# A decoder step with a 32-expert MoE: gathering the routed tokens in slot order, and copying out the windows of experts 0 and 1 in between

## The chip, the core and the metric

The kernel runs on one core of one Trainium2 chip. The metric is the device time of one execution in microseconds. Before the change three runs took 748.0, 749.03 and 749.11 us, with a median of 749.03 us. All of the kernel works on float32 data. Where it wants matmul precision it splits a value into a rounded high part (type fp32r) and the low remainder, and adds three products (high by high, low by high, high by low).

## The reference, cut to what matters

304 tokens (16 meta tokens and 256 prompt tokens, 8 times 4 sample tokens) of 1024 channels pass a mixer, and then a mixture of 32 experts in 4 groups. Only the mixture matters here:

```python
def _hier_moe(xn, ...):
    gidx = top_k(gl, 1)                      # one group of 4 for each token
    ev, eidx = lax.top_k(el_sel, 2)          # two experts of the 8 in the group
    combine = one_hot(flat_idx) * weights    # two weights for each token
    for e in range(N_EXPERTS):               # 32
        he = silu(xf @ w_exp_gate[e]) * (xf @ w_exp_up[e])   # 1024 -> 256, twice
        y = y + combine[:, e:e + 1] * (he @ w_exp_down[e])   # 256 -> 1024
```

## The kernel before, in words

**Stages.** The mixer takes the first 358 us of the span. Then come the router (logits, ranks, positions), the selection, the 32 experts, and a tail that picks each token's two result rows from memory, adds them and normalises.

**Slots.** Each token goes to two experts, so there are SLOTS = 608 pairs. The pairs are laid out by expert: expert 0's tokens first, then expert 1's. An expert has at most C = 96 slots in one pass. `off_i` holds the slot at which each expert's tokens begin.

**Selection** (PE: function `gathers`, line 1460). A 0/1 matrix `sel` (304 tokens in 3 row tiles by 608 slots, made by VectorE at lines 1167 and 1168) is multiplied with the normalised tokens, so that slot columns come out as `xs`, 8 channel chunks by 608 slots. A chunk of 304 columns, half of the slots, fits one PSUM bank, so there are 16 steps q: 8 channel chunks by 2 halves. Each step takes 6 matmuls (3 token tiles, high and low part). The steps use banks 0 to 3 in turn. The first four steps run tile by tile as `sel` arrives; step q from 4 on waits (`gat_done`, line 1480) until ScalarE has copied step q - 4 out. ScalarE's copy (line 803) multiplies by the norm's gain and writes `xs`. Before the change, q // 2 is the channel chunk and q % 2 the half, so an expert's columns are complete only after the last step.

**Windows.** An expert's 96 columns, all 8 chunks, are then copied from `xs` at the slot read from `off_i` (a register load, line 785) as `xe_hi` on ScalarE (`window`, line 788), and VectorE subtracts to get `xe_lo` (line 1203, helper line 1189). There are two buffers of each, by e % 2. Before the change, `sel` lies in the same memory as the two `xe_hi` buffers, so these can't be written while a gather still reads `sel`.

**Weights.** For each expert SyncE loads gate, up and down, 1 MB each, into a ring of 4 slots. ScalarE rounds gate and up into `hi_gu[e % 2]` (`split_gate_up`, line 777, two halves), VectorE subtracts into `lo_gu` (line 1189). The same is done to one half of down (`split_down`).

**Order around the change.** Each engine has a list written out by hand, and waits in order:

- ScalarE: `split_gate_up(0)`, `split_down(0)`, `split_gate_up(1)`, the 16 copies, two register loads, `window(0)`, `window(1)`, then the loop over experts, where each turn starts with Silu of the gate (line 814).
- VectorE: a wait for `sel`, `split_gate_up(0)`, `split_down(0)`, `split_gate_up(1)`, `window(0)`, `window(1)`, then the loop, where each turn starts with the product of Silu and up (`hid`, line 1215).
- PE: the gathers, then `gate_up(0)` (line 1498, 24 matmuls of 512 columns), `turn(0)` (two transposes of `hid`, line 1510), `gate_up(1)`, `down(0)` (line 1523), `turn(1)`, `gate_up(2)`, and so on. `gate_up(0)` and `gate_up(1)` wait for all 16 copies (`gat_done`, line 1492), for the expert's `xe_lo` (line 1493) and for its `lo_gu` (line 1496).
- SyncE: expert 3's weights once the last gather is done (line 382), and expert e + 4's gate and up once `gate_up(e)` is done (line 387).

Of the kernel before, what the change touches and what calls it, by code (L numbers as in the profile page):

```python
# [9 lines left out]
ACT = mybir.ActivationFunctionType  # L10
# [8 lines left out]
KT = D // P  # L19
# [4 lines left out]
T = TP + NS * TS  # L24
ROWS = (P, P, T - 2 * P)
NT = len(ROWS)
# [12 lines left out]
SLOTS = 2 * T  # L39
# [12 lines left out]
LRU_C = 8.0  # L52
WORK = 19616
MAX_PASSES = -(-T // C)
PLACE_STEPS = 17
ST_DMAS = 6 + NS
WO_BANKS = (0, 1, 2, 3, 6, 7)
# [4 lines left out]
GU_WORDS = KT * 2 * F  # L62
# [20 lines left out]
def trunk(nc, a, o):  # L83
    with ExitStack() as ctx:
# [9 lines left out]
        def rounded(name, buf, at, n):  # L94

            return nc.alloc_sbuf_tensor_at(name, [P, n], F32R, offset=start[buf] + 4 * at)[:, :]
# [4 lines left out]
        bank = [ctx.enter_context(nc.psum_tensor(f"bank{i}", [P, 512], F32))[:, :] for i in range(8)]  # L101
# [4 lines left out]
        work = sb("work", WORK)  # L106
# [38 lines left out]
        xs, xT2 = chan(xs_f), chan(xs_f[:, 0:KT * T])  # L145
        at_hi = KT * XS
# [4 lines left out]
        junk = work[:, at_hi + D:at_hi + 2 * D]  # L151
        at_xe = at_hi + 2 * GU_WORDS + 2 * D
        xe_hi = [rounded(f"xe_hi{b}", "work", at_xe + b * KT * C, KT * C).rearrange("p (k n) -> p k n", k=KT) for b in range(2)]
        sel = rounded("sel", "work", at_xe, NT * SLOTS).rearrange("p (t n) -> p t n", t=NT)
        cut(NT * SLOTS)
        logit = cut((NG + NE) * NT).rearrange("p (t e) -> p t e", t=NT)
        el, oh1, oh2, rank, inw, rtmp = (cut(NE * NT).rearrange("p (t e) -> p t e", t=NT) for _ in range(6))
# [55 lines left out]
        g2_row = par[:, KT * (NG + NE):KT * (NG + NE) + KT]  # L213
# [332 lines left out]
        def _(act):  # L546
# [197 lines left out]
            for t in range(NT + 1):  # L744
# [6 lines left out]
                j = 2 * t + 1  # L751
# [18 lines left out]
            def experts(r):  # L770

                def split_gate_up(e):
                    s = e % EXP_SLOTS
                    act.wait_ge(gu_in[s], r * (32 * NE // EXP_SLOTS) + 32 * (e // EXP_SLOTS) + 32)
                    for q in range(2):
                        k = slice(q * HK, q * HK + HK)
                        nc.scalar.activation(hi_gu[e % 2][:, k], w_gu[s][:, k], ACT.Copy).then_inc(ehi_gu, 1)  # L777

                def split_down(e):
                    s = e % EXP_SLOTS  # L780
                    act.wait_ge(dn_in[s], r * (16 * NE // EXP_SLOTS) + 16 * (e // EXP_SLOTS) + 16)
                    nc.scalar.activation(hi_dn[e % 2], w_dn[s][:, 0], ACT.Copy).then_inc(ehi_dn, 1)

                def first_token(e):
                    return act.value_load(off_i[0:1, e:e + 1], min_val=0, max_val=SLOTS)

                def window(e, at):
                    nc.scalar.activation(xe_hi[e % 2], xs[:, :, bass.ds(at, C)], ACT.Copy).then_inc(xe_act, 1)  # L788

                def results(e):  # L790
                    act.wait_ge(dn_mm, r * NE + (e + 1))
                    if e:
                        act.wait_ge(row_out, r * (16 * NE) + 16 * e)
                    for n in range(2):
                        ins = nc.scalar.activation(row_st[:, n * 512:(n + 1) * 512], bank[4 + n][0:C], ACT.Copy)  # L795
                    ins.then_inc(row_done, 1)

                split_gate_up(0)
                split_down(0)
                split_gate_up(1)  # L800
                for q in range(2 * KT):
                    act.wait_ge(gat_mm, r * (2 * KT) + (q + 1))
                    nc.scalar.activation(xs[:, q // 2, (q % 2) * T:(q % 2 + 1) * T], bank[q % 4][:, 0:T],
                                         ACT.Copy, scale=g2_row[:, q // 2:q // 2 + 1]).then_inc(gat_done, 1)
                at = [first_token(e) for e in range(2)]
                act.wait_ge(gat_done, r * (2 * KT) + 2 * KT)
                act.wait_ge(tail_done, 1)
                for e in range(2):
                    window(e, at[e])
                for e in range(NE):  # L810
                    act.wait_ge(gu_mm, r * NE + (e + 1))
                    if e:
                        act.wait_ge(hid_done, r * NE + e)
                    nc.scalar.activation(sg2, bank[e % 2][0:C, 0:F], ACT.Silu).then_inc(silu2, 1)
                    if e + 2 < NE:
                        split_gate_up(e + 2)
                    act.wait_ge(th_mm, r * NE + (e + 1))
                    nc.scalar.activation(hT_hi, bank[2][:, 0:C], ACT.Copy)
                    nc.scalar.activation(hT_f, bank[2][:, C:2 * C], ACT.Copy).then_inc(hT_act, 1)
                    if e:  # L820
                        results(e - 1)
                    if e + 2 < NE:
                        window(e + 2, first_token(e + 2))
                    if e + 1 < NE:
                        split_down(e + 1)
                results(NE - 1)
# [24 lines left out]
        def _(dve):  # L851
# [43 lines left out]
            e, z, z2, q = lam[:, 0], lam[:, 3], lam[:, 4], lam[:, 1]  # L895
# [14 lines left out]
            for s in range(NS):  # L910
                dve.wait_ge(cst_T, s // 2 + 1)
                at = GLP + s * GLS
# [205 lines left out]
            for t in range(NT):  # L1118
                ins = vec.scalar_tensor_tensor(logit[0:ROWS[t], t], bank[(5, 6, 7)[t]][0:ROWS[t], 0:NG + NE],
                                               stat[0:ROWS[t], 9 + t:10 + t], rbias[0:ROWS[t]], ALU.mult, ALU.add)  # L1120
# [64 lines left out]
            def experts(r):  # L1185

                def split(part, whole, high, done, n, out_done):
                    dve.wait_ge(done, n)
                    vec.tensor_tensor(part, whole, as_f32(high), ALU.subtract).then_inc(out_done, 1)  # L1189

                def split_gate_up(e):
                    s = e % EXP_SLOTS
                    for q in range(2):
                        k = slice(q * HK, q * HK + HK)
                        split(lo_gu[s][:, k], w_gu[s][:, k], hi_gu[e % 2][:, k], ehi_gu, r * (2 * NE) + (2 * e + q + 1), elo_gu)

                def split_down(e):
                    s = e % EXP_SLOTS
                    split(lo_dn[s], w_dn[s][:, 0], hi_dn[e % 2], ehi_dn, r * NE + (e + 1), elo_dn)

                def window(e):
                    at = dve.value_load(off_i[0:1, e:e + 1], min_val=0, max_val=SLOTS)
                    split(xe_lo[e % 2], xs[:, :, bass.ds(at, C)], xe_hi[e % 2], xe_act, r * NE + (e + 1), xe_dve)

                dve.wait_ge(sel_done, r * NT + NT)
                split_gate_up(0)
                split_down(0)
                split_gate_up(1)
                window(0)
                window(1)  # L1210
                for e in range(NE):
                    dve.wait_ge(silu2, r * NE + (e + 1))
                    if e:
                        dve.wait_ge(th_mm, r * NE + e)
                    vec.tensor_tensor(hid, bank[e % 2][0:C, F:2 * F], sg2, ALU.mult).then_inc(hid_done, 1)
                    if e + 2 < NE:
                        split_gate_up(e + 2)
                    dve.wait_ge(hT_act, r * NE + (e + 1))
                    vec.tensor_tensor(hT_lo, bank[2][:, 0:C], as_f32(hT_hi), ALU.subtract).then_inc(hT_dve, 1)
                    if e + 2 < NE:  # L1220
                        window(e + 2)
                    if e + 1 < NE:
                        split_down(e + 1)
# [56 lines left out]
        def _(pe):  # L1280
# [179 lines left out]
            def gathers(r):  # L1460

                def gather(q, t):

                    n = ROWS[t]
                    for part in (xn2_hi, xn2_lo):
                        ins = mm(bank[q % 4][:, 0:T], part[t][0:n].rearrange("p (m j) -> p j m", j=KT)[:, q // 2],  # L1466
                                 sel[0:n, t, (q % 2) * T:(q % 2 + 1) * T],
                                 start=(t == 0 and part is xn2_hi), stop=(t == NT - 1 and part is xn2_lo))
                    return ins

                pe.wait_ge(hi_done, r * NT + NT)
                pe.wait_ge(lo_done, r * NT + NT)
                for t in range(NT):
                    pe.wait_ge(sel_done, r * NT + (t + 1))
                    for q in range(4):
                        ins = gather(q, t)
                        if t == NT - 1:
                            ins.then_inc(gat_mm, 1)
                for q in range(4, 2 * KT):
                    pe.wait_ge(gat_done, r * (2 * KT) + (q - 3))  # L1480
                    for t in range(NT):
                        ins = gather(q, t)
                    ins.then_inc(gat_mm, 1)
# [79 lines left out]
```

## Time and profile before

| what | value |
|---|---|
| median of 3 runs | 749.03 us (748.0 to 749.11) |
| the profiled execution | 748.74 us |
| its span in the trace | 747.0 us, so 1.74 us lie around the span |
| mean granted clock of PE | 0.911 of full speed |
| PE busy | 665.1 us, 89% of the span |
| VectorE busy | 539.4 us, 72% |
| ScalarE busy | 368.1 us, 49% |
| DMA | 160.29 MB, 215 GB/s over the span |

Starts are counted in us from the span's start. A wait stands in square brackets behind the instruction that waited, with the time and what ended it. PEld is the weight load in front of a matmul. The granted clock is 1.00 at 2.4 GHz and 0.50 at 1.2 GHz. Ends of matmuls are modelled, so the distance between the starts of two of them is the safer reading.

### The profile page before, as it was taken

To read this page: it belongs to the slowest core of one execution; us is meant where nothing else is said; L and a number is where in the kernel's file an instruction comes from. 1 tells how busy PE (TensorE), PEld (TensorE's weight loads), DVE (VectorE), ACT (ScalarE), POOL (GpSimd) and SP (SyncE) were. 2 spreads that over 40 slices of the span, in tenths; PEclk is the share of its full clock that TensorE was granted. 3 is DMA by queue.
4 is the path that set the end of the run, shared out by engine and by line. 5 is a ranking of instruction groups with operands and counts; after the bars stand their busy time and mean duration, and the time that the engine had idled before them with its cause. 6 is when DMAs were issued, how large, how long until landed. Compare 5 with 4: busy or idle time off the path is not lost.

```text
span 747.0 us, 8243 instructions
## 1 busy us (share of the span) xinstructions
PE 665.1 (89%) x3004; PEld 497.6 (67%) x3004; DVE 539.4 (72%) x739; ACT 368.1 (49%) x515; POOL 134.8 (18%) x102
## 2 busy tenths in 40 slices
PE   5999998992976979999999899999999999999920
PEld 5677776771966879987697566666666666666610
DVE  2079987898999999752287067877788888887406
ACT  2120115443721516540263267778777778778421
POOL 1019852062674500210000000000000000000030
PEclk8699999996897989999686599999999999999975
DMA  9756053333041323440700379999999999998143
GB/s 269 212 179 225 7 219 113 112 113 113 23 149 55 117 109 124 134 169 0 309 29 0 120 291 365 397 399 396 398 403 409 396 395 406 402 395 314 43 148 123
DMA packets 46054, 160.29 MB, mean 215 GB/s; under 512 B 7566, under 2 KB 10870, under 8 KB 33702
## 3 DMA queue, kind: packets, MB, share of 16 engines
q1 hardware_dynamic: 37152, 153.99, 54.5%
q10 hardware_dynamic: 8150, 3.21, 2.1%
q0 software_dynamic: 704, 2.49, 1.0%
q8 instruction: 26, 0.43, 0.2%
q14 instruction: 22, 0.18, 0.1%
HBM read 145.51 MB, written 15.02 MB: 215 GB/s over the span
## 4 chain that ended last, share of the span: by engine, by line
PE 55%; DVE 5%; issue 2%; DMA 1%; ACT 1%; POOL 0%; POOLq 0%; DVEq 0%; ACTq 0%
PE bank L1498 24%; PE bank L1523 13%; PE bank L1414 4%; PE bank L1466 4%; PE bank L1344 4%; PE bank L1286 2%; PE bank L1429 1%; DVE w_lo L995 1%; DMA ring<-expert_rows,row_i 1%; PE bank L1510 1%; PE bank L1441 1%; DVE x L1261 1%; DVE conv L1037 1%; DVE gel_lo L995 0%; DVE work L990 0%
## 5 line engine op out<-in xcount | busy, mean ns | idle before, releaser
L1189 DVE TENSOR_TENSOR lo_gu<-ring,hi_gu 128x2048 fp32r<-128x2048 f32 x64 | 143.8, 2288 | 39.9 <-ACT hi_gu L777 39.9
L1349 PE MATMUL bank<-work,ring 128*128 128x304 f32 x512 | 135.5, 426 | 1.0 <-ACT work L576 1.0
L927 DVE SCALAR_TENSOR_TENSOR work<-work,par 128x272 f32<-128x272 f32 x240 | 131.7, 620 | 0.0
L1349 PEld LDWEIGHTS bank<-work,ring 128*128 128x128 f32 x512 | 98.8, 193 | 35.8 <-issue 3.0
L777 ACT ACTIVATE hi_gu<-ring 128x2048 fp32r<-128x2048 f32 x64 | 118.5, 1901 | 0.0
L1498 PE MATMUL bank<-hi_gu,xe_hi 128*96 128x512 f32 x256 | 103.9, 406 | 3.6 <-issue 3.6
L1498 PE MATMUL bank<-lo_gu,xe_hi 128*96 128x512 f32 x256 | 101.6, 397 | 0.0
L1498 PE MATMUL bank<-hi_gu,xe_lo 128*96 128x512 f32 x256 | 101.2, 395 | 0.0
L530 POOL DMA_INDIRECT ring<-expert_rows,row_i x6 | 5.7, 953 | 346.7 <-DMA expert_rows<-outst 345.2
L1344 PE MATMUL bank<-xn_hi,w_hi 128*128 128x304 f32 x128 | 41.7, 326 | 26.6 <-DVE xn_lo L995 15.1
L1523 PE MATMUL bank<-ring,windows 128*96 128x512 f32 x128 | 65.3, 591 | 0.0
L1498 PEld LDWEIGHTS bank<-hi_gu,xe_hi 128*96 128x96 f32 x256 | 42.7, 167 | 19.8 <-issue 3.9
L453 POOL TENSOR_TENSOR work<-ring 128x272 f32<-128x272 f32 x8 | 45.8, 5722 | 52.4 <-ACT ring L602 52.4
L1498 PEld LDWEIGHTS bank<-lo_gu,xe_hi 128*96 128x96 f32 x256 | 41.5, 162 | 18.7
L1498 PEld LDWEIGHTS bank<-hi_gu,xe_lo 128*96 128x96 f32 x256 | 41.9, 164 | 16.1
L995 DVE TENSOR_TENSOR w_lo<-ring,w_hi 128x2048 fp32r<-128x2048 f32 x17 | 40.2, 2370 | 14.7 <-ACT w_hi L657 14.7
L657 ACT ACTIVATE w_hi<-ring 128x2048 fp32r<-128x2048 f32 x20 | 38.1, 1909 | 20.8 <-PE bank L1344 9.7
L1189 DVE TENSOR_TENSOR xe_lo<-work,xe_hi 128x768 fp32r<-128x768 f32 x32 | 30.4, 952 | 20.4 <-ACT xe_hi L788 20.2
L1344 PEld LDWEIGHTS bank<-xn_hi,w_hi 128*128 128x128 f32 x128 | 26.7, 208 | 27.5 <-issue 27.5
L795 ACT ACTIVATE outst<-bank 96x512 f32<-96x512 f32 x64 | 34.6, 592 | 17.6 <-DMA expert_rows<-outst 13.9
L1344 PE MATMUL bank<-xn_lo,w_hi 128*128 128x304 f32 x128 | 41.4, 323 | 0.0
L1344 PE MATMUL bank<-xn_hi,w_lo 128*128 128x304 f32 x128 | 41.1, 321 | 0.0
(271 smaller groups left out, 1167.7 us busy)
## 6 DMA issues: line engine op xcount, KB each, us to landing
ring<-w_exp_gate SPq DMA_DIRECT2D x32, 1024.0 KB, 7.1
ring<-w_exp_up SPq DMA_DIRECT2D x32, 1024.0 KB, 9.4
ring<-w_exp_down SPq DMA_DIRECT2D x32, 1024.0 KB, 9.5
ring<-w_in SPq DMA_DIRECT2D x11, 2048.0 KB, 8.3
expert_rows<-outst SPq DMA_DIRECT2D x32, 384.0 KB, 7.6
ring<-w_rnn_proj SPq DMA_DIRECT2D x2, 2048.0 KB, 7.7
ring<-w_conv_proj SPq DMA_DIRECT2D x2, 2048.0 KB, 8.3
ring<-w_out SPq DMA_DIRECT2D x2, 2048.0 KB, 7.6
```

The source lines that it names most:

```text
L453: nc.gpsimd.tensor_tensor(glu[:, c, CW - 1:GLP], cv_sb[:, c % 2, 0:TP], sg_sb[:, c % 2, 0:TP], ALU.mult)
L657: nc.scalar.activation(hi, w, ACT.Copy).then_inc(whi_done, 1)
L777: nc.scalar.activation(hi_gu[e % 2][:, k], w_gu[s][:, k], ACT.Copy).then_inc(ehi_gu, 1)
L795: ins = nc.scalar.activation(row_st[:, n * 512:(n + 1) * 512], bank[4 + n][0:C], ACT.Copy)
L927: ins = vec.scalar_tensor_tensor(y, glu[:, ch, w:w + TP], pcw[:, w, ch:ch + 1], y, ALU.mult, ALU.add)
L995: vec.tensor_tensor(part, value, as_f32(high), ALU.subtract).then_inc(lo_sem, 1)
L1189: vec.tensor_tensor(part, whole, as_f32(high), ALU.subtract).then_inc(out_done, 1)
L1344: ins = mm(bank[m % 4][:, 0:T], w[:, i, cols], xp[i], start=(i == 0 and j == 0), stop=(i == KT - 1 and j == 2))
L1349: ins = mm(bank[m % 4][:, 0:T], mix_w[b % MIX_SLOTS][:, i, (c % MB) * P:(c % MB + 1) * P], xnT[:, i], start=(i == 0), stop=(i == KT - 1))
L1414: ins = mm(bank[q][0:ROWS[t]], xp[:, c, tok], w[:, i], start=(c == 0 and j == 0), stop=(c == KT - 1 and j == 2))
L1498: ins = mm(bank[b][0:C], xp[b][:, k], w[:, k], start=(k == 0 and j == 0), stop=(k == KT - 1 and j == 2))
L1523: ins = mm(bank[4 + n][0:C], hp, w[:, at], start=(j == 0), stop=(j == 3))
```

## The change

The gathers take all 8 channel chunks of the first half of the slots in steps 0 to 7, and those of the second half in steps 8 to 15. `sel` moves from the memory of the `xe_hi` buffers to that of `hi_gu[1]`. ScalarE copies out the windows of experts 0 and 1 behind its copies 9 and 12, each after a wait for the first 8 copies. ScalarE's `split_gate_up(1)` moves behind all 16 copies, since `hi_gu[1]` holds `sel` until then, and the wait for `tail_done` (the zeroed end of `xs`) moves behind that. VectorE's `window(0)` moves ahead of its `split_gate_up(1)`.

```diff
+FIRST_WINDOWS = (9, 12)
...
-        sel = rounded("sel", "work", at_xe, NT * SLOTS).rearrange("p (t n) -> p t n", t=NT)
+        sel = rounded("sel", "work", at_hi + GU_WORDS, NT * SLOTS).rearrange("p (t n) -> p t n", t=NT)
...
                 split_gate_up(0)
                 split_down(0)
-                split_gate_up(1)
                 for q in range(2 * KT):
                     act.wait_ge(gat_mm, r * (2 * KT) + (q + 1))
-                    nc.scalar.activation(xs[:, q // 2, (q % 2) * T:(q % 2 + 1) * T], bank[q % 4][:, 0:T],
-                                         ACT.Copy, scale=g2_row[:, q // 2:q // 2 + 1]).then_inc(gat_done, 1)
-                at = [first_token(e) for e in range(2)]
-                act.wait_ge(gat_done, r * (2 * KT) + 2 * KT)
+                    nc.scalar.activation(xs[:, q % KT, (q // KT) * T:(q // KT + 1) * T], bank[q % 4][:, 0:T],
+                                         ACT.Copy, scale=g2_row[:, q % KT:q % KT + 1]).then_inc(gat_done, 1)
+                    if q in FIRST_WINDOWS:
+                        e = FIRST_WINDOWS.index(q)
+                        at = first_token(e)
+                        act.wait_ge(gat_done, r * (2 * KT) + KT)
+                        window(e, at)
+                split_gate_up(1)
                 act.wait_ge(tail_done, 1)
-                for e in range(2):
-                    window(e, at[e])
...
                 split_down(0)
+                window(0)
                 split_gate_up(1)
-                window(0)
                 window(1)
...
-                        ins = mm(bank[q % 4][:, 0:T], part[t][0:n].rearrange("p (m j) -> p j m", j=KT)[:, q // 2],
-                                 sel[0:n, t, (q % 2) * T:(q % 2 + 1) * T],
+                        ins = mm(bank[q % 4][:, 0:T], part[t][0:n].rearrange("p (m j) -> p j m", j=KT)[:, q % KT],
+                                 sel[0:n, t, (q // KT) * T:(q // KT + 1) * T],
```

## Rows read from the trace of the kernel before

**Rows 1.** The page: PE's busy line, and its granted clock in 40 slices

```profile
PE 665.1 (89%) x3004; PEld 497.6 (67%) x3004; DVE 539.4 (72%) x739; ACT 368.1 (49%) x515; POOL 134.8 (18%) x102
...
PEclk8699999996897989999686599999999999999975
```

**Rows 2.** Chain that ended last, 380 to 460 us: start, length, engine, line

```profile
390.49 32.26 PE bank L1466 x96
...
422.77 0.52 ACT work L803
423.29 3.02 issue
426.32 7.63 PE bank L1498 x24
...
433.97 0.39 ACT gate_weights L814
...
434.38 0.43 DVE gate_weights L1215
...
435.34 5.56 PE bank L1498 x24
```

**Rows 3.** Timeline of ScalarE: start, length, line, operation, count, wait before it

```profile
389.63 3.70 ACT L777 ACTIVATE hi_gu<-ring 128x2048 fp32r<-128x2048 f32 x2
...
409.80 0.51 ACT L803 ACTIVATE work<-bank,par 128x304 f32<-128x304 f32 x1 [1.65 <-PE bank L1466]
411.96 0.51 ACT L803 ACTIVATE work<-bank,par 128x304 f32<-128x304 f32 x1 [1.65 <-PE bank L1466]
414.12 0.51 ACT L803 ACTIVATE work<-bank,par 128x304 f32<-128x304 f32 x1 [1.65 <-PE bank L1466]
...
424.28 1.58 ACT L788 ACTIVATE xe_hi<-work 128x768 fp32r x2 [0.99 <-ACT work L803]
```

**Rows 4.** Timeline of VectorE

```profile
401.88 4.48 DVE L1189 TENSOR_TENSOR lo_gu<-ring,hi_gu 128x2048 fp32r<-128x2048 f32 x2
...
425.26 1.83 DVE L1189 TENSOR_TENSOR xe_lo<-work,xe_hi 128x768 fp32r<-128x768 f32 x2 [18.90 <-ACT xe_hi L788]
...
436.18 4.49 DVE L1189 TENSOR_TENSOR lo_gu<-ring,hi_gu 128x2048 fp32r<-128x2048 f32 x2 [1.38 <-ACT hi_gu L777]
```

**Rows 5.** Timeline of PE's weight loads in one gather step

```profile
407.53 1.03 PEld L1466 LDWEIGHTS bank<-sel,half 128*128 128x128 f32 x4 [0.27 <-issue]
```

**Rows 6.** Timeline of PE in the first gate_up: matmuls 2 and 10

```profile
426.83 0.63 PE L1498 MATMUL bank<-hi_gu,xe_lo 128*96 128x512 f32 x1
...
430.24 0.45 PE L1498 MATMUL bank<-hi_gu,xe_hi 128*96 128x512 f32 x1
```

**Rows 7.** Stretches of PE alone: us, busy (count), granted clock, DMA share, GB/s

```profile
230.27:235.40 5.13, 5.13 (x20) 0.50 0.01 3
235.40:235.90 0.50, 0.50 (x5) 0.62 0.00 0
263.88:269.50 5.62, 5.62 (x22) 0.50 0.55 210
269.50:270.00 0.50, 0.50 (x4) 0.58 0.00 0
...
426.32:430.00 3.68, 3.68 (x9) 0.50 1.02 427
430.00:430.40 0.40, 0.40 (x3) 0.57 0.92 389
```

**Rows 8.** One stretch, all engines: PE, PEld, DVE, ACT, POOL, clock, DMA, GB/s

```profile
462.25:702.15 239.90, 239.90 (x973) 154.53 (x972) 190.85 (x162) 186.54 (x242) 0.00 (x0) 1.00 0.96 377
```

**Rows 9.** Waits of SyncE's DMA queue, 420 to 711 us

```profile
SPq L358 <- PE bank L1498: 86.2, 28, 9.9
```

**Rows 10.** DMA issues, 480 to 560 us and 640 to 690 us: median us to landing

```profile
ring<-w_exp_up SPq DMA_DIRECT2D x9, 1024.0 KB, 9.5
...
ring<-w_exp_up SPq DMA_DIRECT2D x4, 1024.0 KB, 9.2
```

## The prediction

> **What bounds the kernel now.** I read the page first: PE is busy 89% of the span, and its granted clock dips several times, the last of them before the tail at the router and the gathers [rows 1]. Then the chain that ended last, around the selection. From 390.49 us it runs over PE alone: 96 gather matmuls for 32.26 us, then ScalarE's last copy of 0.52 us, then 3.02 us in which the chain names nothing ("issue"), then the first gate_up at 426.32 us [rows 2]. What stands in the 3.02 us is seen in the timelines: ScalarE sits 0.99 us between its last copy and the windows (register loads and a semaphore), makes the two windows from 424.28 us in 1.58 us, and VectorE's `xe_lo` of expert 0 begins at 425.26 us, a pair of them taking 1.83 us [rows 3, 4]. So the windows stand between the gathers and the experts while PE does nothing. After that PE works without a pause: 239.90 us busy of 239.90 us between 462.25 and 702.15 us [rows 8]. Whatever is taken from PE's path ahead of that stretch comes off the end, if nothing gives it back.
>
> **The change, part by part.** The sum is made for the profiled execution, 748.74 us (747.0 us of span and 1.74 us around it); the median of the runs is 0.29 us above it.
>
> *Windows taken off the path.* Expert 0 has at most 96 slots and begins at 0; expert 1 begins by 96, so both windows end by column 192, inside the first half of 304. They are complete after copy 7. `gate_up(0)` then waits only for the last copy, which ends at 423.29 us [rows 2]. How long PE takes from there is a handoff. The trace gives one from ScalarE to VectorE of 0.02 us (433.97 plus 0.39 to 434.38), and the pause of PE's weight loads at a gather step, where the awaited copy was done long before, of 0.27 us [rows 2, 5]. PE has three waits, all but the first met by then. I take 0.10 us, nearer to the first since the gathers' pause comes with a pile of weight loads; the ends are 0.02 and 0.30. PE starts at 423.39 instead of 426.32 us: **-2.9 us** (-3.0 to -2.7).
>
> *The windows' new place.* In the gathers a step takes 2.16 us (0.51 of copy and 1.65 of waiting on ScalarE [rows 3]). Step 9's copy starts at 409.80 us. Behind it come a register load and a window: at most 0.99 us (which held two loads before) and about 0.85 us, since two windows took 1.58. ScalarE is back by 412.2 us, where the next copy was due at 409.80 + 2.16 = 411.96 us: 0.2 us late. PE needs that bank only four steps after it was filled, so three steps cover it, over 6 us. The copy of step 12 starts three steps later, and by the last copy ScalarE is on time: 0. Without this cover the two would cost 2 times 0.2 us. VectorE's `window(0)` falls into its 18.90 us of waiting [rows 4]: 0.
>
> *`split_gate_up(1)` behind the gathers.* On ScalarE it leaves 389.63 us, where it delayed nothing (the first copies wait for PE), and begins at 423.29 us. Two halves take 3.70 us, to 427.0; VectorE follows after the first, 1.9 us later (3.70 over 2), at 425.2 us, takes 4.49 us, to 429.7, and `window(1)` adds 0.95 us (half of 1.83, rounded up), to 430.6 [rows 3, 4]. What hides it is `gate_up(0)`, 7.63 us. From 423.39 it ends at 431.0; Silu and `hid` follow as before, with VectorE wanted for `hid` 0.43 us after that (426.32 + 7.63 to 434.38 [rows 2]), at 431.5. VectorE is free 0.9 us earlier. Behind the moved work on ScalarE stands Silu, which can't begin before 431.0 either, 4 us after ScalarE is done; behind it on VectorE stands only `hid`. `gate_up(1)` starts 1.4 us after the end of `gate_up(0)`, 1.8 us after `window(1)` is done. Cost 0; if the cover were gone (ScalarE's 3.70, VectorE's last half of 2.25 and 0.95 in the open after `gate_up(0)`) it would be 6.9 less 1.4 us.
>
> *The order of the gathers, and `sel`'s place.* The same 96 matmuls, shapes and banks, only other chunks of the same tiles. In the old order every second step repeats the chunk of the step before; step 10 brings a new one and step 11 repeats it, and both copies come 2.16 us after the one before (409.80, 411.96, 414.12 [rows 3]). So a new chunk in every step costs nothing and gains nothing: 0. No row shows `sel` at another address; with the same reads of it, 0 as well.
>
> *SyncE.* Expert 3's weights still leave after the last gather; loads 4 and later follow `gate_up` and shift with it. Nothing is passed on a queue.
>
> *The clock.* PE runs at 0.50 through the gathers and into `gate_up(0)`. In the stretch from 430.00 to 430.40 us the mean is 0.57, so the rise came 0.06 us before its end, at 430.34 (0.07 of the 0.50 between the levels, times 0.40 us), 4.02 us after the first matmul [rows 7]. At the low level a matmul takes (430.24 - 426.83) / 8 = 0.426 us, at the high one 5.56 / 24 = 0.232 us [rows 6, 2], so each us of low clock costs 1 - 0.232/0.426 = 0.46 us. I take the same 4.02 us after the new start. Two other starts after idle time rose later: 235.78 less 230.27 is 5.51 us, 269.92 less 263.88 is 6.04 us [rows 7]. At 6.04 us, 2.02 later, it would cost 0.9 us. An earlier rise can gain at most 0.9 us too, since then `hid` waits for VectorE, which is free at 430.6 only.
>
> Sum: 748.74 - 2.9 = 745.8 us for the profiled execution, **746.1 us** against the median.
>
> **The rule weighed against it.** The forecast ties the rise to the start of the dense work; the rows show a rise 4.02, 5.51 and 6.04 us after three such starts, so it is not one fixed delay [rows 7]. The Trainium skill (TensorE: Matmul & The Clock Gate, section "Part 1: The HAM clock gate", "What's actually happening") says that the watch on PE's activity runs freely and does not start anew with a kernel, so that the point of the rise varies. By that rule the three unequal delays are what one would see, and an earlier start need not bring an earlier rise.
>
> **Rivals.**
>
> 1. *The rise stays where it was, at 430.34 us.* Then `gate_up(0)` runs 430.34 - 423.39 = 6.95 us low instead of 4.02: 2.93 times 0.46 = 1.35 us given back, a gain of 1.6, **747.5 us**. For it: the unequal delays. Against: 6.95 us is longer than each of the three delays seen. The Trainium skill (TensorE: Matmul & The Clock Gate, the section named above) would allow it.
>
> 2. *VectorE becomes the bound.* If its chain runs 1.8 us later than worked out (it would start after both of ScalarE's halves, at 427.0), it ends at 432.4 and `hid` begins 0.9 us late: **747.0 us**. Against: VectorE's pair follows ScalarE's first half after 1.38 us of waiting in the expert loop, half by half [rows 4].
>
> 3. *DMA sets the pace of the experts, and gives the gain back:* **749.0 us**, no change. For it: the DMA share is 0.96 at 377 GB/s over the expert stretch [rows 8]. Against: SyncE waits 86.2 us for PE over 28 loads, so PE's progress releases them, and the time to landing does not grow along the stage, 9.5 then 9.2 us [rows 9, 10]; PE has no idle time there [rows 8].
>
> 4. *Slower: the clock does not rise in `gate_up(0)` at all.* All 24 matmuls at 0.426 take 10.2 us, 2.6 more than 7.63; after the 1.4 us pause `gate_up(1)` starts low as well, and 4.02 us at 0.46 costs 1.8 more. With the gain of 2.9 that is +1.5 us, **750.6 us**. It decides from a rise later than 4.02 + 2.9/0.46 = 10.3 us after the start, about when `gate_up(0)` would end. For it: the gathers leave the clock low, and they now run up to 0.6 us before the dense work. Against: the rise came in 4 to 6 us each time.
>
> That the change doesn't do what it says is ruled out by the columns: both windows lie in the first half.
>
> **How the numbers follow.** Chances: the forecast, with the rise 3 to 6 us after the start, 0.74; rival 1 0.10; rival 2 0.07; rival 3 0.06; rival 4 0.03. The forecast's own ends: 746.1 less 0.9 (early rise) and 0.1 (handoff) is 745.1; plus 0.9 (late rise) and 0.2 (handoff) is 747.2. Rival 1's 747.5 is taken in, so the range is 745.1 to 747.5; half of rival 1, rivals 3 and 4 and some scatter (the runs of before lie within 1.1 us) stay outside. A measurement of this kernel tells about 0.2%, 1.5 us, from no change, so the border is 747.5: the forecast, rival 2 and half of rival 1 lie under it, 0.86, of which 0.01 goes off for scatter: 0.85 for faster; rival 3, the other half and the scatter are the same, 0.12; rival 4 is slower, 0.03.
>
> **What would show it.** In the changed trace: the copies of steps 9 and 12 followed by one window each, the next copy late by some 0.2 us and no wait of PE for it; between the last copy and the first line-1498 matmul 0.1 us instead of 3.02; `lo_gu` of expert 1 and its `xe_lo` done on VectorE before `hid`; the rise of the clock some 4 us behind the new start; PE without idle time in the experts, and the tail as long as before. It would be wrong if the gathers took longer than 32.3 us, if idle time showed ahead of the first Silu, `hid` or `gate_up(1)`, or if waits on expert loads appeared.

## The result, and the profile after

The first comparison gave a median of 743.42 us over 6 runs (742.28 to 745.31) against 748.05 us for the kernel before (6 runs, 747.17 to 749.11), a ratio of 0.994 with a 95% interval of 0.9921 to 0.9958. The change is faster, as forecast, but the time lies below the range of 745.1 to 747.5 us. The profiled execution took 742.31 us, with a span of 740.6 us.

The chain of waits of the changed kernel from the gathers to the second expert (start, length, engine, line), the answer to [rows 2]. Lines 1466, 1498, 814 and 1215 of the kernel before are 1468, 1500, 816 and 1217 here:

```profile
388.49 31.89 PE bank L1468 x96
...
420.40 0.52 ACT work L803
420.92 0.04 issue
420.97 7.45 PE bank L1500 x24
...
428.50 0.39 ACT gate_weights L816
...
428.91 0.43 DVE gate_weights L1217
...
429.87 5.56 PE bank L1500 x24
```

The 3.02 us of "issue" have become 0.04. That is the whole of what the change sets out to do, and it is done. But the first gather starts at 388.49 us and not at 390.49, after code that the change does not touch. The difference of the two spans, 6.4 us, splits like this: 2.0 ahead of the first gather, 0.4 in the gathers, 3.0 in the pause, 0.2 in the first gate_up, and 0.9 behind the start of the second one (747.0 - 435.34 = 311.7 before, 740.6 - 429.87 = 310.7 after). Only the third of these was forecast. Each is the difference of one profile and another; further profiles of both kernels follow below.

ScalarE's timeline in the changed kernel, the answer to [rows 3] (step 9, its window, steps 10 to 12, the second window, steps 13 to 15, and `split_gate_up(1)`):

```profile
407.42 0.51 ACT L803 ACTIVATE work<-bank,par 128x304 f32<-128x304 f32 x1 [1.65 <-PE bank L1468]
408.32 0.84 ACT L789 ACTIVATE xe_hi<-work 128x768 fp32r x1 [0.39 <-ACT work L803]
409.59 0.52 ACT L803 ACTIVATE work<-bank,par 128x304 f32<-128x304 f32 x1 [0.42 <-PE bank L1468]
...
414.56 0.84 ACT L789 ACTIVATE xe_hi<-work 128x768 fp32r x1
416.07 0.51 ACT L803 ACTIVATE work<-bank,par 128x304 f32<-128x304 f32 x1 [0.67 <-PE bank L1468]
...
420.40 0.51 ACT L803 ACTIVATE work<-bank,par 128x304 f32<-128x304 f32 x1 [1.65 <-PE bank L1468]
420.81 3.70 ACT L778 ACTIVATE hi_gu<-ring 128x2048 fp32r<-128x2048 f32 x2
```

Behind the first window ScalarE still waits 0.42 us for PE: the next copy is on time, since one register load leaves 0.39 us of idle time and not 0.99. VectorE's answer to [rows 4]:

```profile
422.75 4.49 DVE L1191 TENSOR_TENSOR lo_gu<-ring,hi_gu 128x2048 fp32r<-128x2048 f32 x2 [12.48 <-ACT hi_gu L778]
427.16 0.95 DVE L1191 TENSOR_TENSOR xe_lo<-work,xe_hi 128x768 fp32r<-128x768 f32 x1
428.91 0.42 DVE L1217 TENSOR_TENSOR gate_weights<-bank,gate_weights 96x256 f32<-96x256 f32 x1 [0.80 <-ACT gate_weights L816]
```

VectorE waits 0.80 us for Silu ahead of `hid`: the moved split is hidden, where 0.9 us of room had been worked out. The expert stage is as before (240.00 us busy of 240.00 us on PE), the answer to [rows 8]:

```profile
424.00:424.80 0.80, 0.80 (x4) 0.51 (x3) 0.80 (x1) 0.52 (x1) 0.00 (x0) 0.65 1.04 430
...
456.77:696.77 240.00, 240.00 (x974) 154.57 (x974) 190.97 (x162) 186.68 (x243) 0.00 (x0) 1.00 0.95 376
```

The first row of that fence answers to [rows 7]: a mean clock of 0.65 over 0.80 us puts the rise at 424.80 less 0.24, 424.56 us, 3.59 us after the first matmul of gate_up, where 4.02 was taken.

So the question of the study is the 1.7 us between the 2.9 forecast and the 4.6 measured. Two theories stood against each other. **Scatter**: the change is worth its pause, and the rest is where the clock happens to rise and fall in stretches that it does not touch. **Local**: the change itself gains 4 to 5 us.

### The profile page after: what moved, and what is told of

It reads as the page before. It is cut to its first block, busy times and chain, and to the rows that moved or that the text cites. A ratio compares the mean times of both kernels' runs of the same rounds, so it can differ in the third digit from the quotient of the medians.

```text
span 740.6 us, 8243 instructions
## 1 busy us (share of the span) xinstructions
PE 659.3 (89%) x3004; PEld 492.8 (67%) x3004; DVE 539.8 (73%) x739; ACT 368.2 (50%) x515; POOL 135.8 (18%) x102
## 4 chain that ended last, share of the span: by engine, by line
PE 59%; DVE 3%; DMA 1%; issue 1%; ACT 0%; POOL 0%; POOLq 0%; DVEq 0%; ACTq 0%
PE bank L1500 24%; PE bank L1525 14%; PE bank L1346 7%; PE bank L1416 5%; PE bank L1468 4%; PE bank L1288 2%; PE bank L1431 1%; DMA ring<-expert_rows,row_i 1%; PE bank L1512 1%; PE bank L1443 1%; DVE x L1263 1%; DVE conv L1039 1%; DVE gel_lo L997 0%; DVE x L1277 0%; POOL ring L531 0%
## 5 line engine op out<-in xcount | busy, mean ns | idle before, releaser
L1191 DVE TENSOR_TENSOR lo_dn<-ring,hi_dn 128x1024 fp32r<-128x1024 f32 x32 | 39.0, 1218 | 1.7 <-ACT hi_dn L783 1.7
L1346 PE MATMUL bank<-xn_hi,w_lo 128*128 128x304 f32 x128 | 39.9, 312 | 0.0
```

What stands on the lines that cost most here:

```text
L1346: ins = mm(bank[m % 4][:, 0:T], w[:, i, cols], xp[i], start=(i == 0 and j == 0), stop=(i == KT - 1 and j == 2))
```

## Experiments

### The two kernels again

The kernel before, run again as if it were a change:

> The kernel before, unchanged, with a profile of its own. Scatter theory (the change is worth 2.9 us at the handoff, the rest of the 4.6 us measured is where the granted clock happens to rise and fall in stretches the change does not touch): ratio 1.000, single times scattered over 1 to 3 us as in the runs before; the first gather starts at another time than 390.49 us, by up to 2 us, and the stretch from the first gather to the end of the first gate_up is 43.5 us within 1. Local theory (the change itself is worth 4 to 5 us, between the first gather and the end of the first gate_up): the first gather starts within 0.3 us of 390.49 and the stretch is 43.5 us within 0.3.

Measured: 748.36 us (745.65 to 750.12, 12 runs), ratio 1.0009 (0.9994 to 1.0023). Its first gather starts at 389.59 us, 0.9 us ahead of the same code in the profile before, and 43.4 us pass from there to the end of the first gate_up.

> The changed kernel, unchanged, with a profile of its own. Scatter theory: ratio 0.9955 to 0.9965 (2.6 to 3.4 us); the pause between the last copy and the first gate_up 0.05 us; the stretch from the first gather to the end of the first gate_up 40.5 us within 1; the start of the first gather not tied to 388.5 us. Local theory: ratio 0.993 to 0.995 (4 to 5 us), the stretch below 39.5 us, and the first gather as in the kernel before.

Measured: 745.34 us (742.16 to 748.13, 10 runs), ratio 0.9957 (0.9941 to 0.9974), which is 3.2 us. The chain of its profile:

```profile
390.33 32.28 PE bank L1468 x96
...
422.63 0.52 ACT work L803
423.15 0.04 issue
423.20 7.42 PE bank L1500 x24
```

The pause is 0.04 us here too, but the first gather starts at 390.33 us: the 2 us ahead of the gathers did not come from the change. A third comparison of both:

> The changed kernel a third time. Scatter theory: ratio 0.9945 to 0.9965, so that over all its runs it stays at 3.0 to 3.6 us; the profile has a pause of 0.05 us ahead of the first gate_up, and single times spread over 3 us or more. Local theory: ratio 0.9925 to 0.9945, as the 4.6 us of the first comparison.

Measured: 745.45 us (743.78 to 747.74, 12 runs), ratio 0.9972 (0.9957 to 0.9987): less than expected, on the other side of the forecast from the first comparison. Its pause is 0.04 us again, its first gather at 390.57 us.

> The kernel before a third time, as a measure of the scatter. Scatter theory: ratio 1.000 within 0.0015, single times over 3 us or more; its first gather starts between 388 and 391 us, and a span is short where that start is early. Local theory: the first gather at 390.5 within 0.3.

Measured: 747.31 us (745.37 to 749.19), ratio 0.9995 (0.998 to 1.001), first gather at 390.18 us. Its pause and the gate_up behind it:

```profile
422.45 0.52 ACT work L803
422.97 3.02 issue
425.99 7.66 PE bank L1498 x24
```

All runs of the two kernels in this study (119 of the kernel before, those beside the experiments below among them, and 28 of the changed one) have means of 747.90 and 745.03 us: **2.9 us**. Standard deviations of single runs are 1.4 and 1.5 us, so that difference is uncertain by some 0.6 us (twice the root of 1.4 squared over 119 plus 1.5 squared over 28). By the means of each comparison for itself it is 4.5, 2.8 and 2.0 us; the two repeats together, without the first that they were to check, give 2.4. The intervals of the first and the third comparison barely touch, so one comparison is somewhat less certain than its own interval says.

The traces measure the change with less of that scatter. From the first gather to the end of the first gate_up it takes 43.5, 43.4 and 43.5 us in the three profiles of the kernel before, and 39.9, 40.3 and 40.4 in those of the changed one: 3.2 us less, within what the scatter theory said (40.5 within 1) and above the 39.5 that the local theory allowed. The local theory falls by this.

### The parts of the change, one at a time

The order of gathers and copies alone, on the kernel before:

```diff
-  xs[:, q // 2, (q % 2) * T:...]   and   j=KT)[:, q // 2], sel[0:n, t, (q % 2) * T:...]
+  xs[:, q % KT, (q // KT) * T:...] and   j=KT)[:, q % KT], sel[0:n, t, (q // KT) * T:...]
```

> The order of the gathers and of their copies alone; sel, the windows and the splits stay where they were. Scatter theory: ratio 1.000 within 0.002, gather stretch 32.3 us within 0.9, pause ahead of the first gate_up 3.0 us. A rival, that the new order itself makes the gathers cheaper (a fresh chunk at each step): ratio 0.998 or less, and the gathers under 31.4 us.

Measured: ratio 0.9992 (0.9976 to 1.0008), gathers 32.14 us, pause 3.02 us. The order alone is worth nothing that can be told.

The changed kernel with the windows behind the copies again:

```diff
-                    if q in FIRST_WINDOWS:
...
-                        window(e, at)
-                split_gate_up(1)
-                act.wait_ge(tail_done, 1)
+                at = [first_token(e) for e in range(2)]
+                act.wait_ge(gat_done, r * (2 * KT) + 2 * KT)
+                act.wait_ge(tail_done, 1)
+                for e in range(2):
+                    window(e, at[e])
+                split_gate_up(1)
```

> The changed kernel, with the two windows put back behind the 16 copies, and split_gate_up(1) behind them. Scatter theory: the 3.0 us pause is back, split_gate_up(1) stays hidden under the first gate_up; ratio to the kernel before 1.000 within 0.002. Rival, that moving sel and split_gate_up(1) is itself worth something: ratio 0.998 or less; rival, that the moved split costs: ratio above 1.002 with VectorE late for hid.

Measured: ratio 0.9998 (0.9982 to 1.0014). Its chain:

```profile
388.57 31.86 PE bank L1467 x96
...
420.97 3.02 issue
423.99 7.63 PE bank L1499 x24
```

The pause is back and the gain is gone, though this profiled execution is a short one (745.58 us) with an early first gather, at 388.57 us. So an early start of the gathers happens without the change's windows as well. The windows' place is the part that counts; order and memory only allow it.

The windows five and three steps later:

```diff
-FIRST_WINDOWS = (9, 12)
+FIRST_WINDOWS = (14, 15)
```

> The changed kernel with the two windows behind copies 14 and 15 instead of 9 and 12. Cover theory (a window costs nothing as long as it ends ahead of the next copy's due time): the window of expert 0 fits between copies 14 and 15, that of expert 1 stands behind the last copy and pushes split_gate_up(1) back by 1.2 us, so that VectorE is 0.3 us late for hid: ratio to the kernel before 0.9955 to 0.997, as the changed kernel within its scatter. Rival, that a window between the copies holds up the gathers: the last gather 0.5 us or more later than in the changed kernel, counted from the first.

Measured: ratio 0.9953 (0.9935 to 0.997), as the changed kernel; from the first gather to the start of the last copy it takes 32.3 us (422.63 - 390.33), as in the repeats of the changed kernel, so a window between the copies holds up nothing in the gathers. But expert 0's `xe_lo` now ends at 423.31 us (422.35 and 0.96), 0.17 behind the last copy, and the first gate_up starts at 423.41 us, 0.27 behind it instead of 0.04. The cover of the split is used up, as its chain shows:

```profile
428.47 1.90 issue
430.37 0.95 DVE xe_lo L1191
431.32 0.34 DVE gate_weights L1217
```

VectorE's `window(1)` now stands in the chain directly ahead of `hid`; with Silu over at 431.20 us (430.82 and 0.38) it is late by about 0.1 us, less than the 0.3 expected.

### The pause itself

Four copies of no use ahead of the windows of the kernel before:

```diff
+                for i in range(4 if isinstance(r, int) else 0):
+                    nc.scalar.activation(xe_hi[i % 2], xs[:, :, 0:C], ACT.Copy).then_inc(extra, 1)
+                    act.wait_ge(extra, i + 1)
                 for e in range(2):
                     window(e, at[e])
```

> The kernel before with four useless copies of windows, one after the other, ahead of the two that count, so that the pause behind the gathers is about 4 us longer (0.85 us and a semaphore each). Theory that PE's pause costs its own length and no more: ratio 1.0045 to 1.006, first gate_up 7.4 to 8.5 us as before. Rival, that a longer pause also makes the clock rise later: ratio above 1.006 and a first gate_up over 8.5 us. Rival, that a pause is given back in the expert stage: ratio below 1.003.

Measured: 752.19 us, ratio 1.0057 (1.004 to 1.0074), 3.0 to 5.5 us slower. The pause grew from 3.02 to 6.54 us, that is by 3.52:

```profile
424.06 6.54 issue
430.60 8.12 PE bank L1502 x24
```

The interval holds the 3.5 us, and the first gate_up of 8.12 us is what the order-only kernel had too (426.40 to 434.52 us) behind a pause of 3.02. So a longer pause costs its length; that it costs some tenths more by a later rise of the clock is not excluded by that interval.

The other way round, PE kept at work in the pause of the kernel before:

```diff
                     ins.then_inc(gat_mm, 1)
+                keep_clock(7, 12)
```

> The kernel before, with 12 small matmuls of no use behind the last gather, so that PE works through most of the 3.0 us pause. Theory that the pause costs its own length only: the first gate_up starts at the same distance from the last gather, and the ratio is 1.000 to 0.997, the latter where the clock rises within the filled pause and the first gate_up takes 5.6 us instead of 7.6. Rival, that an idle pause in itself holds the clock down longer: the first gate_up at 5.6 to 6.2 us every time and ratio 0.997 or less, which would be 1.4 to 2 us that the change gains beside the pause.

Measured: ratio 0.9993 (0.9976 to 1.001). Its chain, and PE's clock in the filled stretch:

```profile
388.65 31.84 PE bank L1466 x96
420.49 4.81 PE bank L1286 x24
425.30 5.57 PE bank L1499 x24
```

```profile
420.42:424.00 3.58, 3.58 (x18) 0.50 0.66 227
424.00:425.06 1.06, 1.06 (x10) 0.76 0.98 410
```

The small matmuls (24 on PE, two for each of the 12) took 4.81 us, 1.3 longer than the pause and the copy together (3.54), and gate_up took 2.1 us less. The clock rose at about 424.5 us, some 4.1 us after the filling began, as late as it does behind the start of a gate_up. So the rise came some 4 us behind the start of this work, ahead of gate_up. What this leaves, 0.8 us, is within the interval; the experiment does not settle whether the idle time adds a few tenths to the delay.

### Where single runs differ

Useless matmuls at the start of the changed kernel, 40 instead of 24, so that the clock might stay up until the first tiles:

```diff
-            keep_clock(2, 24)
+            keep_clock(2, 40)
```

> The changed kernel with 40 instead of 24 small matmuls of no use at the very start, which fill PE's 6 us of waiting ahead of the first transposes. Scatter theory (single times differ because the clock rises sooner or later at several starts, of which the one at 25 us is the first): if the clock stays at 1.00 up to 25 us, the first tiles run at the high level from their start, the first gather comes 1.5 to 2.4 us earlier and the ratio to the kernel before is 0.992 to 0.995. Rival: the transposes and waits between 16 and 25 us let the clock fall all the same, and the ratio is that of the changed kernel, 0.9955 to 0.997.

Measured: ratio 0.9954 (0.9936 to 0.9971), as the changed kernel. The clock was at 0.50 from 16 us on all the same, under the transposes: the rival holds, and this run says nothing for or against the scatter theory.

What does show a source of the scatter is the router stage of three profiles, all with the same instructions there. Its transposes in the changed kernel, in the same kernel again, and in the order-only kernel (shortest, median and longest in ns, then the first and the last start):

```profile
L1443 PE MATMUL bank<-ident,x x24: 274/339/477, 358.2 to 369.3; 128*128 128x128 f32 x16, 48*128 48x48 f32 x8
```

```profile
L1443 PE MATMUL bank<-ident,x x24: 274/357/477, 358.8 to 370.8; 128*128 128x128 f32 x16, 48*128 48x48 f32 x8
```

```profile
L1441 PE MATMUL bank<-ident,x x24: 274/375/477, 357.7 to 370.3; 128*128 128x128 f32 x16, 48*128 48x48 f32 x8
```

The stage takes 30.3, 31.5 and 33.0 us up to the first gather (388.49, 390.33 and 390.70). PE's clock in it, in the same order (from 360 to 365 and from 375 to 380 us; the fourth number):

```profile
360.00:365.00 5.00, 5.00 (x29) 0.81 1.02 428
...
375.00:380.00 5.00, 5.00 (x39) 0.82 0.01 3
```

```profile
360.00:365.00 5.00, 5.00 (x25) 0.69 1.00 421
...
375.00:380.00 5.00, 5.00 (x29) 0.60 0.01 5
```

```profile
360.00:365.00 5.00, 5.00 (x22) 0.50 1.01 424
...
375.00:380.00 5.00, 5.00 (x26) 0.50 0.00 0
```

The later the clock falls and the earlier it rises, the shorter the stage, by up to 2.7 us, about the whole spread between the profiles. The other profiles of kernels with this stage agree, twelve in all: where the clock's mean from 375 to 380 us is 0.82 or 0.83, the first gather starts at 388.49 to 388.65 us (three: the changed kernel's first, and the kernels with the late windows and with the filled pause, which have the windows behind the gathers); at 0.56 to 0.69 it starts at 389.59 to 390.57 (six), and at 0.50 at 390.70 to 391.40 (three). The gathers follow too: 31.84 to 31.89 us in the first three, 32.12 to 32.31 in the others. So the 2.0 and the 0.4 us of the first pair of profiles come without the change as well. Other sources of the scatter, some 1.5 us ahead of 190 us and about 1 us behind the second gate_up (2 us more in the filled kernel's profile, where the tail's fetch of result rows and the wait ahead of it were longer), were not followed up.

### A version that beats both

The gathers' weight loads read every eighth value of a token. Writing the normalised tokens chunk by chunk makes them neighbours:

```diff
-  nc.scalar.activation(xn2_hi[t][0:n], x[0:n, t], ACT.Copy, ...
+  nc.scalar.activation(xn2_hi[t][0:n].rearrange("p (j m) -> p m j", j=KT),
+                       x[0:n, t].rearrange("p (m j) -> p m j", j=KT), ACT.Copy, ...
...
-  part[t][0:n].rearrange("p (m j) -> p j m", j=KT)[:, ...]
+  part[t][0:n].rearrange("p (j m) -> p j m", j=KT)[:, ...]
```

(`xn2_lo` likewise.) First on the kernel before:

> The kernel before, with the normalised tokens written chunk by chunk, so that a gather's weight load reads 128 neighbouring values instead of every eighth. Theory that the strided weight load paces the gathers (0.337 us of load for each of 96) and that its gaps are what let the clock fall: load 0.20 us, clock stays at 1.00, gathers 14 to 16 us instead of 32.3, first gate_up 5.6 us, ratio 0.973 to 0.980. Rival, that the load's length is set by something else than its stride: gathers 32 us, ratio 1.000.

Measured: 738.23 us, ratio 0.9861 (0.9834 to 0.9887). Then on the changed one:

> The changed kernel with the same chunk-by-chunk tokens. If the pause and the weight load are separate costs: ratio to the kernel before 0.969 to 0.976. With gathers of 15 us and a first gate_up of 5.6 us the cover of split_gate_up(1) is gone: VectorE should end window(1) about 1.3 us after hid wants it, so the gain over the dense kernel before is 1 to 2 us instead of 3. Rival: the split stays hidden and the gain over it is 3 us or more.

Measured: 736.28 us (732.44 to 737.38), ratio **0.9834** (0.9803 to 0.9864), 2.0 us by the medians below the dense kernel before (3.1 by the means, uncertain by some 2 us, so that six runs each do not tell the expected 1 to 2 us from 3). Its profile is that of its fastest run, 732.44 us. Weight loads of the gathers in this kernel, and the chain:

```profile
L1470 PEld LDWEIGHTS bank<-sel,half x96: 182/187/192, 391.4 to 409.6; 128*128 128x128 f32 x64, 48*128 48x128 f32 x32
```

```profile
391.49 18.59 PE bank L1470 x96
410.11 0.53 ACT work L804
410.68 7.37 PE bank L1502 x24
```

A load takes 0.187 us where it took 0.337, the gathers 18.6 us where they took 32.3, and the clock stays at 1.00 from 395 to 410 us, where it was 0.50 from 400 on. The clock is not what made the strided load long: in the kernel before it took 0.337 us on average from 388 to 396 us, at 1.00, and 0.332 from 400 to 420, at 0.50. Both gains were expected larger. The loads still fill the steps (1.12 us for six in a step of 1.16), and the scattered writing costs 2.03 us instead of 1.13 for each of ScalarE's three high parts and 2.00 instead of 1.28 for each of VectorE's low parts, which also read the high part at that step, on the way to the gathers. That the split's cover would be gone did not come about: the clock fell once more behind the gathers, gate_up took 7.37 us, and VectorE had 0.72 us left.

## Why the prediction was right in its mechanism and wrong in its time

**Windows off the path: right.** 2.9 us was forecast for the pause; it fell from 3.02 to 0.04 us in three profiles of three, so 2.98. The handoff taken at 0.10 us was 0.04. With the windows put back the gain is gone. That the gain of all runs, 2.9 us, agrees with the forecast to the tenth is luck: it is uncertain by 0.6, the repeats alone give 2.4, and the traces 3.2.

**The windows' new place: right.** The 0.2 us of delay came from counting two register loads; one copy later ScalarE was waiting for PE.

**The split's cover: right**, 0.80 us against 0.9, and used up where the split starts 1.2 us later.

**The clock in the first gate_up: right within its bounds.** The rise came 3.59 us after the start and gate_up took 7.45, 7.42 and 7.50 us (7.86 with the 40 matmuls at the start), against 7.63, 7.51 and 7.66 in the kernel before: some tenths, at the edge of what these profiles can tell. Rival 1, a rise at an unmoved time, falls: it rose at 424.56 us, not at 430.34. In eleven profiles (the filled pause and the two with shorter weight loads apart) the rise came 3.6 to 5.1 us after the first gate_up began, not 6.95. The order-only kernel's 8.12 us behind the same pause, from the same instructions, shows that the delay differs from run to run. What it does to the time is scatter, not a loss of the gain. The Trainium skill (TensorE: Matmul & The Clock Gate, "Part 1: The HAM clock gate", "What's actually happening") says that the watch on PE's activity runs freely, so that the point of the rise varies; the 7.42 to 8.12 us agree.

**A reading that was wrong: "PE runs at 0.50 through the gathers".** The mean clock of the kernel before was 1.00 from 390 to 395 us and 0.62 from 395 to 400, so it fell at 396.2 us, 5.7 us into the gathers. No term of the sum hung on it, but the time of this fall is one of the things that differ from run to run: in the changed kernel's first profile the mean from 395 to 400 us was 0.73, a fall 8.8 us into the gathers, and they took 0.4 us less.

**Rivals 2 to 4** did not happen: `hid` waits for Silu, PE has no idle time in the experts, and the clock rose within gate_up.

**The step that failed is the range, in the words "half of rival 1, rivals 3 and 4 and some scatter (the runs of before lie within 1.1 us) stay outside": a term for the scatter was put at nothing.** Three runs were taken for the scatter, and their median, 749.03 us, for the level. Over 119 runs the kernel before goes from 745.22 to 752.27 us, with a median of 747.94, 1.1 us below that level. And the changed kernel's six first runs, 742.28 to 745.31 us, lay low in its own spread (742.16 to 748.13 over 28 runs, mean 745.03). So 746.1 was 1.1 us too high by its starting level, and the remaining 1.6 us of the miss are how far the first comparison lies below that mean. That this second part is the chance of six runs is not shown: their mean is 743.65 us, that of the 22 later ones 745.41, and a trace was kept of one of the six, which is of the group with the earliest first gather. The prediction itself put what a measurement can tell at 1.5 us, for its border between faster and the same, and left it out of the range; with it the range would have begun at 743.6, near the 743.42 measured. The range should have carried a term for the clock at each stage that starts low, the router's 2.7 us first, and not only for the stage that the change touches. The trace of before showed these stages [rows 1]; they were read as fixed.

## What to carry to other kernels

Where an engine idles between two stages for the sake of the first item of the second, order the first stage so that this item's input is complete early, and make the copy in its waiting time; look for memory that the two share, since that, not the order alone, holds the copy back. Before a range of a few tenths of a per cent is given, take the spread from many runs, or from how many stages start at a low clock, and not from three. Look at the length of a weight load with a stride beside that of one without: here the stage with 0.337 us a load fell to a clock of 0.50 in all twelve profiles, and with 0.187 us it stayed at 1.00 to its end in both.

## What the runs showed of the hardware that was not expected

The same instructions took 30.3 to 33.0 us in the router stage, and its profiles differ in where the clock fell and rose. A weight load of 128 columns with a step of 32 bytes took 0.337 us and one without a step 0.187. The Trainium skill (SBUF — State Buffer, the note on "cachelines") says that for four-byte values a step of up to four values is free and each access to a new 16-byte line pays; a step of eight values that costs 0.15 us agrees. Writing 1024 values with a step of 512 bytes cost ScalarE 2.03 us instead of 1.13; writing and reading at that step cost VectorE 2.00 instead of 1.28.
